# Convolution sums, gated results and the norm row kept in PSUM in the mixer of a two-block transformer kernel

## The reference

```
proj = u @ w_in;  a_b, a_c, a_v, z, xbc, dt_raw, g_a, g_b = split(proj)
y_a  = (a_b * causal_dwconv3(a_c * a_v)) @ w_out_a
xbc  = silu(causal_dwconv4(xbc) + conv_b);  xs, B, C = split(xbc)
y    = ssd_chunked(xs, softplus(dt_raw + bias), -exp(a_log), B, C) + d_skip * xs
yg   = y * silu(z);  yg = yg * rsqrt(mean(yg^2 over each of 4 groups) + eps) * norm_g
h    = h + (sigmoid(g_a) * y_a + sigmoid(g_b) * (yg @ w_out_ssm)) @ w_mix_out
```

## Time and profile before

| | |
|---|---|
| runs | 1344.98, 1346.03, 1346.53 us (median 1346.03) |
| the profiled execution | 1346.82 us; its span from first to last instruction 1345.0 us |
| mean granted TensorE clock | 0.978 |
| TensorE matmul busy | 1289.0 us (96%) |
| VectorE, ScalarE, GpSimd busy | 724.5, 668.3, 1013.3 us |
| the mixer | about 645 to 1040 us of the span |

### The profile page before, as it was taken

One profiled execution on the slowest core, in us unless ns is written; L12 is line 12 of the kernel. 1 busy time (PEld: TensorE's weight loads), 2 busy tenths in 40 slices (PEclk: granted clock), 3 DMA queues, 4 the chain that ended last, 5 costly groups with the idle time before them and its releaser, 6 DMA issues.

```text
span 1345.0 us, 24723 instructions
## 1 busy us (share of the span) xinstructions
PE 1289.0 (96%) x10187; PEld 1230.6 (92%) x10187; DVE 724.5 (54%) x1293; ACT 668.3 (50%) x1184; POOL 1013.3 (75%) x774
## 2 busy tenths in 40 slices
PE   6989998998998999999999998999999999999997
PEld 6978888987888999999899997889999899999997
DVE  5577746668666443421597687955045434344412
ACT  5445545453554544444544556565436445544532
POOL 4655657766467899888689866667999847898894
PEclk9989998998998999999899999999999999999998
DMA  6433434543334555555455533334555534555552
GB/s 238 133 125 111 126 114 139 165 133 126 111 126 145 173 174 190 182 188 185 130 172 190 187 126 126 111 128 155 189 185 208 166 116 142 173 190 186 188 189 79
DMA packets 57791, 209.05 MB, mean 155 GB/s; under 512 B 6352, under 2 KB 7632, under 8 KB 57424
## 3 DMA queue, kind: packets, MB, share of 16 engines
q1 hardware_dynamic: 57680, 207.48, 46.9%
HBM read 206.41 MB, written 1.05 MB: 154 GB/s over the span
## 4 chain that ended last, share of the span: by engine, by line
PE 80%; DVE 15%; ACT 3%; issue 1%; DMA 1%; SPq 0%; DVEq 0%
PE bank L338 24%; PE bank L340 23%; PE bank L339 23%; PE bank L806 2%; DVE ar L1544 1%; DVE yl L1222 1%; DVE ar L1231 1%; DVE ar L779 1%; PE bank L596 1%; ACT whi L303 1%; DVE ar L1565 1%; PE bank L814 1%; DVE ar L1678 1%; DVE ar L1694 1%; DVE rows L395 1%
## 5 line engine op out<-in xcount | busy, mean ns | idle before, releaser
L311 POOL TENSOR_TENSOR wlo<-raw,whi 128x512 fp32r<-128x512 f32 x770 | 1013.1, 1347 | 315.4 <-ACT whi L303 314.9
L338 PE MATMUL bank<-xh,whi 128*128 128x256 f32 (+1 forms) x2024 | 588.2, 291 | 13.9 <-DVE xl L377 9.0
L340 PE MATMUL bank<-xh,wlo 128*128 128x256 f32 (+1 forms) x2024 | 577.6, 285 | 0.0
L339 PE MATMUL bank<-xl,whi 128*128 128x256 f32 (+1 forms) x2024 | 577.3, 285 | 0.0
L303 ACT ACTIVATE whi<-raw 128x1024 fp32r<-128x1024 f32 x387 | 398.7, 1049 | 43.8 <-DMA raw<-w_dram 21.7
L338 PEld LDWEIGHTS bank<-xh,whi 128*128 128x128 f32 x2024 | 388.4, 192 | 23.7 <-issue 13.8
L340 PEld LDWEIGHTS bank<-xh,wlo 128*128 128x128 f32 x2024 | 388.7, 192 | 0.0
L339 PEld LDWEIGHTS bank<-xl,whi 128*128 128x128 f32 x2024 | 387.4, 191 | 0.5
L338 PE MATMUL bank<-yh,whi 128*128 128x256 f32 (+1 forms) x1000 | 288.5, 288 | 8.8 <-DVE yl L1222 8.4
L339 PE MATMUL bank<-yl,whi 128*128 128x256 f32 (+1 forms) x1000 | 285.3, 285 | 0.0
L340 PE MATMUL bank<-yh,wlo 128*128 128x256 f32 (+1 forms) x1000 | 285.1, 285 | 0.0
(11 more groups left out here) (244 smaller groups left out, 1217.5 us busy)
## 6 DMA issues: line engine op xcount, KB each, us to landing
raw<-w_dram SPq DMA_DIRECT2D x387, 512.0 KB, 3.7
h<-x_dram SPq DMA_DIRECT2D x2, 544.0 KB, 5.6
cst<-con_dram SPq DMA_DIRECT2D x1, 1049.0 KB, 9.9
ar<-mem_dram SPq DMA_DIRECT2D x1, 1024.0 KB, 5.9
out_dram<-h SPq DMA_DIRECT2D x4, 256.0 KB, 2.7
cst<-con_dram SPq DMA_DIRECT2D x1, 134.0 KB, 3.7
prm<-par_dram SPq DMA_DIRECT2D x1, 131.0 KB, 4.1
```

What stands on the lines that cost most here:

```text
L311: return e.tensor_tensor(wlo[:, q, c0:c1], raw[:, i % NRAW, c0:c1], whi[:, q, c0:c1].bitcast(F), ALU.subtract)
L338: e.matmul(o, wh, xhi, start=(i == 0), stop=False)
L339: e.matmul(o, wh, xlo, start=False, stop=False)
L340: m = e.matmul(o, wl, xhi, start=False, stop=(i == len(feed) - 1))
```

## The change

- `short_vector`: the product c·v is written to columns 256 to 511 of the `av` bank and read from there; the `cin` buffers with their zeroed margins go, the shifted sums are written to shortened ranges instead. The gated result goes to the upper half of the `ab` bank, which stays taken until the low half is made (`ya`).
- `taps`: the order of the four taps is reversed, a copy of the bias fills the first three columns, and the last tap writes the sum into the upper half of the `cv` bank. ScalarE's tanh and VectorE's gate read it there; the bank stays taken until `cvx`.
- The causally masked C·B product `cbm` is made in place in the bank `cb`, which stays taken until the last head pair has used it (`MC`, g, 3).
- The skip sum `yd` is written back to its bank, and the product with z reads it there; the bank stays taken until `yz`.
- The norm row is read from its bank `gr`; ScalarE's copy goes; the bank stays taken until the fourth `yn`.
- The gate `os` and the merged sum stay in the `os` bank until `mg2` is split.
- In the `z` loop `silu_vector` and `silu_scalar` of the last pair come ahead of the work on z.

```diff
             o = main.take(e, *name)[:, 0:n]
-            main.give(name, (by, name))
+            main.give(name, *(by if isinstance(by, list) else [(by, name)]))
...
-    cin, cv, mtmp = ring("cin", [ci0, ci1, ci2]), ring("cv", [cv0, cv1, cv2]), ring("mtmp", [mt0, mt1, mt2])
+    cv, mtmp = ring("cv", [cv0, cv1, cv2]), ring("mtmp", [mt0, mt1, mt2])
...
-    grow = rows[0][:, 0:S]
...
     def short_vector(e, j, side):
+        m, c = mtmp.at("short", j), main.at("av", j)[:, S:2 * S]
         e.wait_ge(*product.of("av", j))
-        m = mtmp.at("short", j)
         e.wait_ge(*s_out.of("ac", j))
-        e.tensor_tensor(ci[:, 3:3 + S], m, main.at("av", j)[:, 0:S], ALU.mult).then_inc(*v_out.done("av", j))
+        e.tensor_tensor(c, m, main.at("av", j)[:, 0:S], ALU.mult).then_inc(*v_step.done("cv", "short", j))
+        e.wait_ge(*v_step.of("cv", "short", j))
+        e.tensor_scalar(m, c, pc("ca", 16 + j), None, ALU.mult).then_inc(*v_step.done("ca", j, 2))
+        e.wait_ge(*v_step.of("ca", j, 2))
+        e.scalar_tensor_tensor(m[:, 1:S], c[:, 0:S - 1], pc("ca", 8 + j), m[:, 1:S], ALU.mult, ALU.add).then_inc(
+            *v_step.done("ca", j, 1))
+        e.wait_ge(*v_step.of("ca", j, 1))
+        e.scalar_tensor_tensor(m[:, 2:S], c[:, 0:S - 2], pc("ca", j), m[:, 2:S], ALU.mult, ALU.add).then_inc(
+            *v_out.done("av", j))
         e.wait_ge(*v_out.of("av", j))
...
         e.wait_ge(*product.of("ab", j))
-        e.tensor_tensor(m, m, main.at("ab", j)[:, 0:S], ALU.mult).then_inc(*v_out.done("ab", j))
+        o = main.at("ab", j)
+        e.tensor_tensor(o[:, S:2 * S], m, o[:, 0:S], ALU.mult).then_inc(*v_out.done("ab", j))
...
     def short_low(e, j):
         hi, lo = yc(16 + j)
         e.wait_ge(*s_high.of("ya", j))
-        e.tensor_tensor(lo, mtmp.at("short", j), hi.bitcast(F), ALU.subtract).then_inc(*v_low.done("ya", j))
+        e.tensor_tensor(lo, main.at("ab", j)[:, S:2 * S], hi.bitcast(F), ALU.subtract).then_inc(*v_low.done("ya", j))
     def short_scalar(e, j):
...
+        mtmp.give(("short", j), (v_out, ("ab", j)))
...
+        e.activation(yc(16 + j)[0], main.at("ab", j)[:, S:2 * S], ACT.Copy).then_inc(*s_high.done("ya", j))
...
             s = cv.take(e, cb)
-            cv.give((cb,), (v_step, ("cvx", cb)))
-            e.wait_ge(*product.of("cv", cb))
-            e.tensor_scalar(s, main.at("cv", cb)[:, 0:S], cwh[:, 72 + cb:73 + cb], cbh[:, cb:cb + 1], ALU.mult,
-                            ALU.add).then_inc(*v_step.done("tap", cb, 3))
-        for i in (2, 1, 0):
+            cv.give((cb,), (v_out, ("cv", cb)))
+            e.tensor_copy(s[:, 0:3], cbh[:, cb:cb + 1].broadcast_to([128, 3])).then_inc(*v_step.done("bias", cb))
+        for i in range(3):
             for cb in cbs:
-                s, d = cv.at(cb), 3 - i
-                e.wait_ge(*v_step.of("tap", cb, i + 1))
-                m = e.scalar_tensor_tensor(s[:, d:S], main.at("cv", cb)[:, 0:S - d], cwh[:, 24 * i + cb:24 * i + cb + 1],
-                                           s[:, d:S], ALU.mult, ALU.add)
-                if i:
-                    m.then_inc(*v_step.done("tap", cb, i))
-                else:
-                    m.then_inc(*v_out.done("cv", cb))
+                s, o, d = cv.at(cb), main.at("cv", cb), 3 - i
+                w = cwh[:, 24 * i + cb:24 * i + cb + 1]
+                if i == 0:
+                    e.wait_ge(*product.of("cv", cb))
+                    e.tensor_scalar(s[:, d:S], o[:, 0:S - d], w, cbh[:, cb:cb + 1], ALU.mult, ALU.add).then_inc(
+                        *v_step.done("tap", cb, i))
+                    continue
+                e.wait_ge(*v_step.of("tap", cb, i - 1))
+                e.scalar_tensor_tensor(s[:, d:S], o[:, 0:S - d], w, s[:, d:S], ALU.mult, ALU.add).then_inc(
+                    *v_step.done("tap", cb, i))
+        for cb in cbs:
+            s, o = cv.at(cb), main.at("cv", cb)
+            e.wait_ge(*v_step.of("tap", cb, 2))
+            e.scalar_tensor_tensor(o[:, S:2 * S], o[:, 0:S], cwh[:, 72 + cb:73 + cb], s, ALU.mult, ALU.add).then_inc(
+                *v_out.done("cv", cb))
     def silu_scalar(e, cbs):
         for cb in cbs:
-            e.activation(dst_of(cb), cv.at(cb), ACT.Tanh).then_inc(*s_step.done("cv", cb))
+            e.activation(dst_of(cb), main.at("cv", cb)[:, S:2 * S], ACT.Tanh).then_inc(*s_step.done("cv", cb))
     def silu_vector(e, cbs):
         for cb in cbs:
             x = dst_of(cb)
             e.wait_ge(*s_step.of("cv", cb))
-            e.scalar_tensor_tensor(x, x, 1.0, cv.at(cb), ALU.add, ALU.mult).then_inc(*v_step.done("cvx", cb))
...
-        side_.give(("cb", g), (v_step, ("cbm", g)))
...
+        side_.give(("cb", g), (v_step, ("MC", g, 3)))
...
-            side_.give(("yd", g, half), (v_step, ("yd", g, 2 * half + 1)))
+            side_.give(("yd", g, half), (v_step, ("yz", g, 2 * half + 1)))
...
-        side_.give(("gr", g), (s_step, ("grow", g)))
+        side_.give(("gr", g), (v_step, ("yn", 4 * g + 3)))
...
-        e.tensor_tensor(cbm, side_.at("cb", g)[:, 0:256].rearrange("p (a b) -> p a b", a=2),
-                        cst[:, C_CM:C_CM + 256].rearrange("p (a b) -> p a b", a=2), ALU.mult).then_inc(
-            *v_step.done("cbm", g))
+        cbm = side_.at("cb", g)[:, 0:256]
+        e.tensor_tensor(cbm, cbm, cst[:, C_CM:C_CM + 256], ALU.mult).then_inc(*v_step.done("cbm", g))
+        yield
+        yield
+        cbb = cbm.unsqueeze(1).broadcast_to([128, 2, 256])
...
-                e.scalar_tensor_tensor(x[:, bb, :], x[:, bb, :], pc("sd", 4 * g + bb), o[:, S * b:S * b + S], ALU.mult,
-                                       ALU.add).then_inc(*v_step.done("yd", g, bb))
+                y = o[:, S * b:S * b + S]
+                e.scalar_tensor_tensor(y, x[:, bb, :], pc("sd", 4 * g + bb), y, ALU.mult, ALU.add).then_inc(
+                    *v_step.done("yd", g, bb))
...
-                e.tensor_tensor(x[:, bb, :], x[:, bb, :], z[:, bb, :], ALU.mult).then_inc(*v_step.done("yz", g, bb))
+                e.tensor_tensor(x[:, bb, :], o[:, S * (bb % 2):S * (bb % 2) + S], z[:, bb, :], ALU.mult).then_inc(
+                    *v_step.done("yz", g, bb))
...
-            e.wait_ge(*s_step.of("grow", g))
+            e.wait_ge(*piece.of("gr", g))
+            grow = side_.at("gr", g)[:, 0:S]
             e.scalar_tensor_tensor(x[:, bb, :], x[:, bb, :], snh[:, 4 * g + bb:4 * g + bb + 1], grow, ALU.mult,
                                    ALU.mult).then_inc(*v_step.done("yn", 4 * g + bb))
...
-        e.wait_ge(*piece.of("gr", g))
-        e.activation(grow, side_.at("gr", g)[:, 0:S], ACT.Copy).then_inc(*s_step.done("grow", g))
...
-            block(e, ("ab", j), "w_in2", 0, 128 * j, src, S)
+            block(e, ("ab", j), "w_in2", 0, 128 * j, src, S, by=[(v_low, ("ya", j))])
...
-                    block(e, ("cv", cb), "w_in2", 0, 5120 + 128 * cb, src, S)
+                    block(e, ("cv", cb), "w_in2", 0, 5120 + 128 * cb, src, S, by=[(v_step, ("cvx", cb))])
...
-            block(e, ("os", b), "w_os", 0, 128 * b, srcb, S)
+            block(e, ("os", b), "w_os", 0, 128 * b, srcb, S, by=[(v_low, ("mg2", b))])
...
+                silu_vector(e, due)
+                due = ()
                 e.wait_ge(*s_step.of("z", b))
                 e.scalar_tensor_tensor(x, x, 1.0, main.at("z", b)[:, 0:S], ALU.add, ALU.mult).then_inc(*v_out.done("z", b))
-                silu_vector(e, due)
-                due = ()
...
+            x, y = main.at("os", b)[:, 0:S], main.at("os", b)[:, S:2 * S]
+            e.scalar_tensor_tensor(x, sgb[b], 1.0, x, ALU.add, ALU.mult).then_inc(*v_out.done("os", b))
             e.wait_ge(*v_out.of("os", b))
+            e.tensor_tensor(y, zacc[:, b, :], x, ALU.add).then_inc(*v_step.done("mg2", b))
...
                 split_for(e, "z", b)
+                silu_scalar(e, due)
+                due = ()
                 e.wait_ge(*product.of("z", b))
...
-                silu_scalar(e, due)
-                due = ()
...
+            e.activation(yc(16 + b)[0], main.at("os", b)[:, S:2 * S], ACT.Copy).then_inc(*s_high.done("mg2", b))```

TensorE's queue where group 0's norm row meets the start of group 1 (blocks 11 and 12 after group 0; `bank4` to `bank7` are the side ring, `bank0` the main bank of block 12). Before:

```order
L1640 MATMUL bank5<-cst 128x128 [waits v_step,s_step]
L1640 MATMUL bank5<-cst 128x128
L1577 MATMUL bank6<-cst,ar 128x128 x4
L1577 MATMUL bank4<-cst,ar 128x128 x4
L1582 MATMUL bank7<-cst,ar 128x128 [waits s_step]
L1585 MATMUL bank7<-ar 128x128 x2
L338 MATMUL bank0<-xh,whi 128x256 [waits wlo_done]
...
L1592 MATMUL bank5<-ar 128x512 [waits v_step,s_out,s_step]
L1605 MATMUL bank6<-acr 128x256 x2
```

31 lines of the change are left out of this document (7 added, 24 removed).

## The result

The changed kernel takes 1356.57 us (median of four runs, 1355.36 to 1357.73); the kernel before, run beside it, 1345.51 (1344.98 to 1346.53). The ratio is 1.0084, with a 95% interval of 1.0071 to 1.0097: slower by 11 us. The profiled execution took 1357.73 us (span 1355.7, before 1345.0), at a mean granted clock of 0.976 (before 0.978).

What follows compares the result with a forecast made beforehand. TensorE, busy 96%, was taken as the bound, losing time only in stops or a lower clock. 12.9 + 5.9 + 1.0 - 10.0 - 3.4 (clock behind old stops) = +6.4 us on 1346.8: 1353.2, as median 1352.4; range 1346 to 1359.

Steps and rivals of the forecast that it cites:

- The new stops: At the state product, TensorE waits for the fourth `yn` between groups: 5.5, 4.8 and 2.6 us, together +12.9 us.
- The clock: Half-speed work behind the waits at the state product: 2.1, 2.1 and 1.7 us, together +5.9 us.
- Rival B: Faster by 3 us, 1343.0: TensorE's clock does not fall behind the waits at the state product; chance 0.07.
- The old stops: TensorE's mixer waits before the sums of squares, for the taps' banks and before a mask all go: -10.0 us.
- The main banks: `cv` banks freed at the gate, one pair later, make TensorE wait at block 7: +1.0 us (0 to 2.8).
- Rival C: Slower by 12 us, 1358: dear bank writes, and later release of `cv` banks stops TensorE in each group; chance 0.15.
- Writes to a bank: VectorE's writes to a bank cost nothing extra; at the high end 0.9 us per chain.
- Rival D: GpSimd stretches bank operands like SBUF ones, so stops stay and the new one is added: 1357; chance 0.03.

Runs made afterwards that it cites:

- row_only: Kernel before, with only the norm row read from its bank, which stays taken until the fourth `yn`; 1360.97 us, 1.0118.
- four_first: Changed kernel, with all four applications of the norm row ahead of the taps and the first two low halves on VectorE; 1337.58 us, 0.9942.
- before_four_first: Kernel before, nothing moved to PSUM, with only VectorE's order changed: all four norm row applications ahead of the taps; 1342.58 us, 0.9984.
- row_bank_later: Changed kernel, with the norm row's bank given back two steps later, so the state product takes another bank; 1341.56 us, 0.997.
- four_first_squares: four_first, with the squares of tiles 2 and 3 written to a `yd` bank and summed in three instructions with one bank operand each; 1333.39 us, 0.9914.
- row_copied: Changed kernel, with ScalarE copying the norm row to SBUF again and that copy freeing its bank; 1344.37 us, 0.9991.

## Why the prediction was right, and where not

The forecast was slower, 1352.4 with a range of 1346 to 1359, for a wait at the state product. That is what happened, 4.2 us more than said.

**The new stops.** Right in place, number and cause: L1595 on L1719, three times. 5.5, 4.8 and 2.6 were predicted, 5.73, 5.74 and 2.50 came. The second is the one mis-sized: from its first `yn` to the end of the fourth 5.9 to 6.9 us were counted (843.49 to between 849.4 and 850.4), and the chain took 7.1, as in group 0 to 1 (798.31 to 805.46 above). That the first came out at 5.73 is partly luck: its chain was counted at 6.1 to 7.0 us and took 7.1 as well, but VectorE started it 1.5 us before TensorE reached the state product, where the trace before had 0.7. The low halves are in it with 2.03 us, above their bound of 1.82: both operands in SBUF, and GpSimd at work. row_only and four_first show the cause from both sides: the part alone gives 14.0 us of stops, and moving the taps and the first low halves behind the fourth `yn` leaves 0.8.

**The clock.** Right in kind, 1.9 too small. The long stops were given the 2.1 us of the one at 329.82; they cost 3.3 and 2.8, and their difference is not explained. Rival B is refuted by the three rows of the changed kernel, all at 0.50 or 0.51. The prediction's argument against it, that all stops from 2.5 us on have such a stretch, doesn't hold in general: the third stop at the state product in row_only (2.50 us, at 904.98), the first before the sums of squares in before_four_first (2.47 us, at 832.06) and the second at block 7 in row_bank_later (2.27 us) go on at a granted clock of 1.00. So the 1.7 us for the short stop was a likely price and not a sure one.

**The old stops: the step that failed.** The prediction says of the stops at L1632 that they "should go", and counts all of the old stops, 10.0 us. Of these 6.1 went. The count took the relief of two groups of instructions and left the next ones in the queue, the sums of squares, at the 0.68 and 0.43 us that the trace showed. That trace had them in a gap of GpSimd. Moved forward they met its work and took 1.35 and 1.38, nearly the same in all four groups. four_first_squares gave these sums a bank operand, and the stops went. This is the largest error in the sum, 3.5 us with the 0.3 at 1009 us set against it. The others are the clock (+1.9), the new stops (+1.1), the main banks (-1.0) and the missing stretch (-1.7).

**The main banks.** Predicted 1.0, measured 0. With the stop at the state product out of the way the same hold goes with two stops of 2.27 and 2.25 us in row_copied, with 1.7 us of clock each, and with none in four_first. TensorE comes to block 7 at the same time in both; VectorE's gate is 2.3 us later in the one. So the hold has no fixed price: it turns VectorE's lateness into a stop. The prediction had put VectorE 0.5 us before to 1.4 us after TensorE, and the bias copies at 0.1 us each, where a stretched pair took 1.31. Rival C had the hold as a mechanism, and in row_copied these stops are what ate the gain.

**Writes to a bank.** Taken at nothing: right. L1693 writes a bank in 470 to 489 ns where the earlier trace rows has 465 to 480 for the same sum written to SBUF.

**Rival D** is refuted, by the durations of L1568, L1698 and L1719 after. By the page of the Trainium skill that the prediction cites, VectorE: DVE Perf Modes, section "The TRN2 errata", a bank source would be 65 ns dearer. The trace disagrees: the row applied from the bank takes 468 ns at the median and from SBUF 478, 464 and 470 at least. Of the Trainium skill, SBUF — State Buffer, section "Who interferes with whom", holds that VectorE with at most one SBUF input outside the two-port modes does not contend with GpSimd. With this the trace agrees for L1568, L1698, L1719 and L1693, which take at most 489 ns. The bias copy (L1535) has one SBUF input too and takes up to 1240 ns; whether it ran in one of the two-port modes no run here shows.
